# Forgetting attention moved into q's weight blocks, its query gate taken off TensorE, and two modulation chunks in other jobs

## The chip, the cores and the metric

The kernel is one program on one core of a Trainium2 chip. The metric is the device time of one execution in microseconds (us). A core has TensorE (PE; PEld is its weight load), VectorE (DVE), ScalarE (ACT), GpSimd (POOL) and SyncE (SP); each runs its own instruction stream in order, and the streams wait for one another by semaphores.

## The reference, cut to what matters

Batch 1, 256 tokens, width 2048, float32. A first block (an S5 state-space layer, then a forgetting-attention layer, "fox") is followed by a second block of two hybrid layers (retention beside latent attention), each modulated by a vector computed from `c`.

```python
# fox layer: 16 heads of 128; k, v, cum from shared_kv
s = einsum('bhqd,bhkd->bhqk', q_i, k) * dh ** -0.5
s = s + c_i[..., :, None] - cum[:, :, None, :]     # c_i: the queries' part of cum
s = where(kpos <= qpos, s, NEG_INF)
p = softmax(s, -1); o = p @ v
o = o * silu(z);  h = h + rmsnorm(o @ w_out, g_post)
# hybrid layer l
mod = silu(c) @ w_mod[l] + b_mod[l]                # 6144 values: shift, scale, gate
h = rms_norm(x, g) * (1 + scale) + shift
...
x = x + gate * out
```

`cum` is the running sum of the log forget gates, per head and token.

## The kernel before

**The weight stream.** Every big product is a job (`u`, `z`, `glu`, `s5out`, `k`, `v`, `f`, `q`, `foxz`, `foxout`, then per hybrid layer `rq`, `rk`, `rv`, `ga`, `rg`, `cq`, `ckv`, `kr`, `mg`, four groups of `uq`, `ukv`, `gb`, then `mlaproj`, `retproj`, `out`), and a job of width 2048 is 16 blocks of 128 output columns. SyncE loads each block's weights (1 MB) into one of four `raw` buffers. ScalarE rounds it to `whi` (L444), VectorE subtracts to get `wlo` (L903), two buffers each. TensorE multiplies, for each of the 16 k tiles, `whi` with `xs` hi and lo together (512 columns, L1562) and `wlo` with `xs` hi (256 columns, L1564) into `acc`. ScalarE copies the second half of `acc` out (`acctmp`, L468), VectorE adds the halves into the destination tile (L953). After block j both then split the weights of block j + 2.

**Side work.** `project(key, side=...)` calls `side(j)` on each engine after block j; this is how small work is laid between blocks. The order on each engine is the order written there.

**The modulation.** `MOD_JOBS` names twelve jobs. While such a job runs, VectorE adds one 128x1024 chunk of `w_mod`, scaled by `c`, per block to `modacc` (`mod_step`, L925; the first step after a `memset`, L940), GpSimd loads the chunks (L423), and at the job's end TensorE waits for the last step, sums `modacc` over partitions with 32 small matmuls into `bank[5]` (L1579), and VectorE adds the bias into `modv` (L962). `before_mod` is one more wait ahead of these matmuls where `bank[5]` is also used by attention. The chunks in order are shift, scale and gate of layer 0 (six), then of layer 1.

**Forgetting attention.** Sixteen heads go through `attend_slot(k)`, a software pipeline: slot k makes the scores of head k + 1 on TensorE (L1790 to L1792), the mask pass, maxima and negation of head k + 1 (L1052 to L1056) and the normalisation of head k (L1060 to L1062) on VectorE, the exponentials (L529) on ScalarE, the transposes of head k - 1 (L1619, L1622) and their copies (L537, L538), the product with v of head k - 2 (L1631, L1632), and its copy into `w3` on VectorE (L1356, which counts `att_stored`). Scores of one head are, for both query blocks of 128, three matmuls: q·k (L1790), the queries' part of `cum` spread over keys (L1791), and minus the keys' part spread over queries (L1792); each takes 128 columns for the first query block and 256 for the second.

All of `q` is projected first. Then ScalarE multiplies `w3` (q) by `FOX_SCALE` in four passes (L748), TensorE waits for these (`q_scaled`), slot -1 runs alone, and slots 0 to 15 follow the 16 blocks of `foxz` (the gate z, into `w1`). The gate is sigmoid (ScalarE, `zsig`, L756) and two multiplications (VectorE, L1035) for each group of four heads, three of them after blocks 7, 11 and 15. After `foxz` come slots 16 and 17, the last group's gate, and the four hi (L768) and four lo (L983) splits of the result into `xs`, which `foxout` reads.

**A pattern used elsewhere.** `glu` (and `mlaproj`, `retproj`) end otherwise: the first three groups of the next input are split during the job's last block (`before_last`), each as soon as TensorE has passed the k tiles that it overwrites (`x_released`, k = 3, 7, 11); the weight split of the last block is held back (`held`, `split_held`) behind the fourth group.

Of the kernel before, what the change touches and what calls it, by code (L numbers as in the profile page):

```python
# [69 lines left out]
MOD_JOBS = [(None, n) for n in ("glu", "s5out", "k", "v", "q", "foxz")] + \  # L70
           [(0, n) for n in ("rv", "ga", "rg", "mg", "mlaproj", "retproj")]
# [42 lines left out]
RELEASES = [(None, "glu"), (None, "f")] + [(l, n) for l in range(2) for n in ("mlaproj", "retproj")]  # L114
OVER = {n: f for n, _, f in NORMS}
SPLIT_GROUPS = dict(SPLITS)

# [3 lines left out]
def hybrid_program(nc, x_t, x_p, wstream, modstream, vecs, s5_adt, s5_b, s5_c, s5_cbd, s5_skip, fox_bf, positions,  # L121
# [3 lines left out]
    with ExitStack() as ctx:  # L125
# [70 lines left out]
        fcum = at("fcum", [P, 5, T], F32, o_cr)  # L196

# [239 lines left out]
        def _(act):  # L437
# [16 lines left out]
            def project(key, side=None, held=False):  # L454
                b0 = JOBS[key][0]

                def one(j, s):
                    piece, whole = pieces(key, j)
                    for t, par, _, q in tiles_of(key, j, s):
# [8 lines left out]
                        act.activation(acctmp[:, par % 2, :], acc[par % 2][:, T:2 * T], ACT.Copy).then_inc(acc_low_copied, 1)  # L468
# [267 lines left out]
            def forget(j):  # L736
# [5 lines left out]
                if j == 1:  # L742
                    act.wait_ge(sem("forget_1p"), 1)
                    act.activation(fcum[0:FOX_H, 1, :], fcum[0:FOX_H, 1, :], ACT.Ln).then_inc(sem("forget_ln"), 1)
            project((None, "q"), side=forget)
            act.wait_ge(acc_summed, JOBS[(None, "foxz")][1])
            for g in range(4):
                act.activation(group(w3)(g), group(w3)(g), ACT.Copy, scale=FOX_SCALE).then_inc(sem("q_scaled"), 1)  # L748
            attend_slot(0, -1, FOX_H)

            def z_gate(g):

                act.wait_ge(acc_summed, JOBS[(None, "foxz")][1] + 4 * g + 4)
                if g:
                    act.wait_ge(sem("silu_used"), g)
                act.activation(zsig[:, :, :], group(w1)(g), ACT.Sigmoid).then_inc(sem("silu_gate"), 1)  # L756

            def fox_side(j):
                attend_slot(0, j, FOX_H)
                if j in (7, 11, 15):  # L760
                    z_gate(j // 4 - 1)
            project((None, "foxz"), side=fox_side)
            attend_slot(0, FOX_H, FOX_H)
            z_gate(3)
            act.wait_ge(acc_done, JOBS[(None, "foxout")][1])
            for g in range(4):
                act.wait_ge(sem("silu_used"), g + 1)
                act.activation(xs[:, 4 * g:4 * g + 4, 0, :], group(w3)(g), ACT.Copy).then_inc(x_hi_done, 1)  # L768
# [3 lines left out]
            for l in range(2):  # L772
                silu0, gates0 = 4 + 8 * l, 8 * l
# [123 lines left out]
        def _(dve):  # L897
# [36 lines left out]
            def project(key, dest, rows=P, side=None, turn=lambda ap: ap, held=False):  # L934
# [7 lines left out]
                def one(j, s):  # L942
# [3 lines left out]
                    for t, par, jt, q in tiles_of(key, j, s):  # L946
                        if piece:
                            lo_piece(*piece, q)
                        if key == (None, "z"):
# [3 lines left out]
                        dve.tensor_tensor(out=dest(jt), in0=turn(acc[par % 2][0:rows, 0:T]), in1=turn(acctmp[0:rows, par % 2, :]),  # L953
                                          op=ALU.add).then_inc(acc_summed, 1)
# [90 lines left out]
            def attend_slot(a0, k, heads, scale, kind, finish):  # L1045

                if k + 1 < heads:
                    i, a = k + 1, a0 + k + 1
                    dve.wait_ge(sem("att_scores"), a + 1)
                    if a >= 2:  # L1050
                        dve.wait_ge(sem("att_turned"), a - 1)
                    link(dve.scalar_tensor_tensor(out=smx[:, i % 2, :], in0=bank[i % 2][:, 0:384], scalar=scale,  # L1052
                                                  in1=mask[:, kind, :], op0=ALU.mult, op1=ALU.add))
# [280 lines left out]
            def forget(j):  # L1334
# [4 lines left out]
                if j == 1:  # L1339
# [4 lines left out]
                    dve.tensor_scalar(F[4], F[2], -1.0, None, ALU.mult).then_inc(sem("cum_ready"), 1)  # L1344
            split_x("pre1", stg_half, xs, 3)
            split_held((None, "f"))
            project((None, "q"), lambda j: tile(w3, j), side=forget)
            dve.wait_ge(sem("masks_loaded"), 16)
# [6 lines left out]
            def fox_slot(k):  # L1355
                attend_slot(0, k, FOX_H, 1.0, 0, lambda i, o: dve.tensor_copy(w3[:, i, :], o))  # L1356

            def z_mul(g):
                dve.wait_ge(sem("att_stored"), 4 * g + 4)
                silu_mul(0, g, group(w1)(g), zsig[:, :, :], group(w3)(g))  # L1360

            def fox_side(j):
                fox_slot(j)
                if j in (7, 11, 15):
                    z_mul(j // 4 - 1)
# [693 lines left out]
```

## Time and profile before

| | us |
|---|---|
| median of three runs | 3378.76 (3378.43 to 3387.96) |
| the profiled execution, its own time | 3377.11 |
| its span, first to last instruction | 3375.4 |
| TensorE busy | 3165.9 (94%) |
| VectorE busy | 2237.6 (66%) |
| ScalarE busy | 1480.8 (44%) |
| the 16 DMA engines, mean rate | 193 GB/s |

Busy time is the union of an engine's instructions; mean granted TensorE clock was 0.976 of full speed (2.4 GHz). A timeline row gives start, duration and, in brackets, how long the engine sat idle before it and what released it. Matmuls overlap, so what one costs is the distance to the start of the next, not its duration.

### The profile page before, as it was taken

How to read it: one execution, taken by the hardware profiler on the slowest of the kernel's cores; microseconds unless marked ns; L12 is line 12 of the kernel's file. 1: busy time of each engine (PE TensorE's matmuls, PEld its weight loads, DVE VectorE, ACT ScalarE, POOL GpSimd, SP SyncE). 2: the span in 40 equal slices, each digit the busy share in tenths (PEclk: the TensorE clock that was granted, in tenths of full speed). 3: DMA queues.
4: the chain of work that ended last, by engine and by line, in shares of the span. 5: the costliest groups of instructions: out<-in, count | busy, mean ns of one | idle time of the engine just before them, and what ended most of it. 6: DMA issues, size and time to landing. Idle time of an engine off the chain costs nothing. (4 is left out here: it accounts for less than half of the span.)

```text
span 3375.4 us, 51760 instructions
## 1 busy us (share of the span) xinstructions
PE 3165.9 (94%) x20984; PEld 2734.9 (81%) x20984; DVE 2237.6 (66%) x2653; ACT 1480.8 (44%) x1843; POOL 108.0 (3%) x206
## 2 busy tenths in 40 slices
PE   6999997999989799999999999989999999999997
PEld 5898886878878688888877778868888887777886
DVE  7687877687674668677766667764555765565564
ACT  5454543344453333344444444433334544444443
POOL 0000000000000000000000000000000000000000
PEclk9999998999999899999999999989999999999999
DMA  5334764767544366656653467645544554344543
GB/s 209 127 112 147 260 245 167 280 249 264 187 160 153 145 219 256 235 213 242 244 187 134 149 250 288 217 181 176 179 157 162 188 199 173 127 150 176 212 175 112
DMA packets 102889, 650.13 MB, mean 193 GB/s; under 512 B 11552, under 2 KB 12704, under 8 KB 38688
## 3 DMA queue, kind: packets, MB, share of 16 engines
q1 hardware_dynamic: 71856, 512.44, 42.3%
q0 software_dynamic: 28528, 105.92, 8.7%
q10 hardware_dynamic: 2304, 28.84, 2.1%
q8 instruction: 157, 2.57, 0.3%
q14 instruction: 44, 0.36, 0.0%
HBM read 632.47 MB, written 14.68 MB: 192 GB/s over the span
## 5 line engine op out<-in xcount | busy, mean ns | idle before, releaser
L1562 PE MATMUL acc<-xs,whi 128*128 128x512 f32 x6960 | 2501.1, 403 | 76.3 <-DVE xs L983 60.2
L1564 PE MATMUL acc<-xs,wlo 128*128 128x256 f32 x6960 | 1957.1, 281 | 0.0
L1562 PEld LDWEIGHTS acc<-xs,whi 128*128 128x128 f32 x6960 | 1315.2, 189 | 407.5 <-issue 59.5
L903 DVE TENSOR_TENSOR wlo<-raw,whi 128x2048 fp32r<-128x2048 f32 x459 | 1051.8, 2292 | 502.0 <-ACT whi L444 501.4
L1564 PEld LDWEIGHTS acc<-xs,wlo 128*128 128x128 f32 x6960 | 1322.8, 190 | 6.2 <-issue 3.6
L444 ACT ACTIVATE whi<-raw 128x2048 fp32r<-128x2048 f32 x459 | 875.2, 1907 | 0.0
L468 ACT ACTIVATE acctmp<-acc 128x256 f32<-128x256 f32 x547 | 208.8, 383 | 1349.6 <-PE acc L1564 1331.4
L953 DVE TENSOR_TENSOR w<-acc,acctmp 128x256 f32<-128x256 f32 (+1 forms) x480 | 206.2, 430 | 462.9 <-ACT acctmp L468 462.3
L925 DVE SCALAR_TENSOR_TENSOR modacc<-modw,cact,modacc 128x1024 f32<-128x1024 f32 x192 | 245.6, 1279 | 16.0 <-DMA modw<-in_modstream 14.7
L423 POOL DMA_DIRECT2D modw<-in_modstream x192 | 101.5, 529 | 1709.7 <-DVE modacc L925 1037.4
L529 ACT ACTIVATE smx<-smx,stat 128x128 f32<-128x128 f32 x96 | 43.0, 448 | 175.6 <-DVE stat L1056 175.6
L1562 PE MATMUL acc<-cks,whi 128*128 128x512 f32 x256 | 92.5, 404 | 10.8 <-DVE wlo L916 10.8
L1557 PE MATMUL acc<-xs,whi 128*128 128x256 f32 x512 | 93.0, 284 | 2.2 <-DVE wlo L903 2.2
L1562 PE MATMUL acc<-cqs,whi 128*128 128x512 f32 x192 | 76.8, 436 | 19.1 <-DVE w L953 10.1
L1557 PEld LDWEIGHTS acc<-xs,whi 128*128 128x128 f32 x512 | 79.7, 192 | 2.5 <-DVE wlo L903 2.4
L1559 PE MATMUL acc<-xs,wlo 128*128 128x256 f32 x256 | 72.4, 283 | 0.0
L1564 PE MATMUL acc<-cks,wlo 128*128 128x256 f32 x256 | 71.7, 280 | 0.0
L1562 PEld LDWEIGHTS acc<-cks,whi 128*128 128x128 f32 x256 | 48.0, 188 | 26.7 <-DVE wlo L916 15.7
L916 DVE TENSOR_TENSOR wlo<-raw,whi 128x512 fp32r<-128x512 f32 (+1 forms) x80 | 63.7, 796 | 8.0 <-ACT whi L451 4.2
L1562 PEld LDWEIGHTS acc<-cqs,whi 128*128 128x128 f32 x192 | 39.7, 207 | 31.0 <-DVE w L953 11.4
L1564 PE MATMUL acc<-cqs,wlo 128*128 128x256 f32 x192 | 57.1, 297 | 0.0
L451 ACT ACTIVATE whi<-raw 128x512 fp32r<-128x512 f32 (+1 forms) x80 | 56.7, 709 | 0.0
(256 smaller groups left out, 2181.9 us busy)
## 6 DMA issues: line engine op xcount, KB each, us to landing
raw<-in_wstream SPq DMA_DIRECT2D x483, 1024.0 KB, 4.8
modw<-in_modstream POOLq DMA_DIRECT2D x192, 512.0 KB, 4.7
residual<-h ACTq DMA_DIRECT2D x2, 2048.0 KB, 6.3
ga_gate<-w ACTq DMA_DIRECT2D x2, 2048.0 KB, 10.9
gated_retention<-w ACTq DMA_DIRECT2D x2, 2048.0 KB, 8.5
w<-gated_retention ACTq DMA_DIRECT2D x2, 2048.0 KB, 8.2
h<-residual ACTq DMA_DIRECT2D x2, 2048.0 KB, 12.6
w<-ga_gate ACTq DMA_DIRECT2D x2, 2048.0 KB, 11.3
```

The source lines that it names most:

```text
L423: pool.dma_start(modw[s][:, :], src).then_inc(mod_loaded[s], 16)
L444: act.activation(whi[s % SPL][:, :], raw[slot][:, :], ACT.Copy).then_inc(w_hi_done, 1)
L451: ins = act.activation(whi[n % SPL][:, c], raw[n % RAW][:, c], ACT.Copy)
L468: act.activation(acctmp[:, par % 2, :], acc[par % 2][:, T:2 * T], ACT.Copy).then_inc(acc_low_copied, 1)
L903: dve.tensor_tensor(out=wlo[s % SPL][:, :], in0=raw[s % RAW][:, :], in1=whi[s % SPL][:, :].bitcast(F32), op=ALU.subtract).then_inc(w_lo_do ...
L916: ins = dve.tensor_tensor(out=wlo[n % SPL][:, c], in0=raw[n % RAW][:, c], in1=whi[n % SPL][:, c].bitcast(F32), op=ALU.subtract)
L925: dve.scalar_tensor_tensor(out=modacc[:, :], in0=modw[s % 2][:, :], scalar=cact[:, bass.ds(j, 1)] if not isinstance(j, int) else cact[:, j ...
L953: dve.tensor_tensor(out=dest(jt), in0=turn(acc[par % 2][0:rows, 0:T]), in1=turn(acctmp[0:rows, par % 2, :]), op=ALU.add).then_inc(acc_summ ...
L1557: pe.matmul(acc[par % 2][:, 0:T], whi[w][:, c:c + cols], x_split[:, k, a, :], start=(k == 0 and a == 0), stop=False, skip_group_check=True)
L1559: mm = pe.matmul(acc[par % 2][:, 0:T], wlo[w][:, c:c + cols], x_split[:, k, 0, :], start=False, stop=(k == kts - 1), skip_group_check=True)
L1562: pe.matmul(acc[par % 2][0:cols, :], whi[w][:, c:c + cols], x_split[:, k, :, :], start=(k == 0), stop=False, skip_group_check=True)
L1564: mm = pe.matmul(acc[par % 2][0:cols, 0:T], wlo[w][:, c:c + cols], x_split[:, k, 0, :], start=False, stop=(k == kts - 1), skip_group_check ...
```

## The change

1. Attention starts after block 3 of `q` (`FOX_FIRST`) with slot -1; slots 0 to 11 follow blocks 4 to 15 of `q`, slots 12 to 17 follow blocks 0 to 5 of `foxz`. TensorE's `q` job is now written out block by block.
2. The scale goes into q's sum (ScalarE's copy of the low half takes `scale`, VectorE's addition becomes a multiply-add), so the four passes L748 and `q_scaled` go.
3. The matmuls L1791 go. Instead TensorE transposes the queries' part of `cum` once (after block 2), VectorE copies 16 columns per query block into `cumcol`, and the mask pass adds its column as a per-partition scalar, in two passes (128 and 256 columns wide) for the former one of 384.
4. The gate of groups 0, 1 and 2 runs after blocks 4, 8 and 12 (ScalarE) and 5, 9 and 13 (VectorE) of `foxz`. In the last block's time the gate of three tiles of group 3 and the splits of groups 0 to 2 are made; the last tile's gate, the fourth group's split and the held weight split follow.
5. `foxz` and layer 0's `rg` no longer carry a modulation chunk; layer 1's `rv` and `mg` do. `before_mod` now stands at the end of `q`: it waits until head 9 is stored.

```diff
-MOD_JOBS = [(None, n) for n in ("glu", "s5out", "k", "v", "q", "foxz")] + \
-           [(0, n) for n in ("rv", "ga", "rg", "mg", "mlaproj", "retproj")]
+MOD_JOBS = [(None, n) for n in ("glu", "s5out", "k", "v", "q")] + \
+           [(0, n) for n in ("rv", "ga", "mg", "mlaproj", "retproj")] + [(1, "rv"), (1, "mg")]
...
+FOX_FIRST = 3
+FOX_SILU = 5
+def fox_slot_at(job, j):
+    return j - FOX_FIRST - 1 if job == "q" else KT - FOX_FIRST - 1 + j
...
# ScalarE
-                        act.activation(acctmp[:, par % 2, :], acc[par % 2][:, T:2 * T], ACT.Copy).then_inc(acc_low_copied, 1)
+                        act.activation(acctmp[:, par % 2, :], acc[par % 2][:, T:2 * T], ACT.Copy,
+                                       scale=FOX_SCALE if key == (None, "q") else 1.0).then_inc(acc_low_copied, 1)
...
-            for g in range(4):
-                act.activation(group(w3)(g), group(w3)(g), ACT.Copy, scale=FOX_SCALE).then_inc(sem("q_scaled"), 1)
...
+            def fox_hi(groups, key):
+                for g in groups:
+                    if key:
+                        act.wait_ge(sem("x_released"), released(key, g))
+                    act.wait_ge(sem("silu_used"), g + 1 if g < 3 else FOX_SILU)
+                    act.activation(xs[:, 4 * g:4 * g + 4, 0, :], group(w3)(g), ACT.Copy).then_inc(x_hi_done, 1)
+            def fox_early():
+                z_gate(3, range(3))
+                fox_hi(range(3), (None, "foxz"))
+            project((None, "foxz"), side=before_last(fox_side, fox_early), held=True)
+            z_gate(3, (3,), 1)
+            split_held((None, "foxz"))
             act.wait_ge(acc_done, JOBS[(None, "foxout")][1])
+            fox_hi((3,), None)
...
# VectorE
+                        if key == (None, "q"):
+                            dve.scalar_tensor_tensor(out=dest(jt), in0=acc[par % 2][:, 0:T], scalar=FOX_SCALE,
+                                                     in1=acctmp[:, par % 2, :], op0=ALU.mult, op1=ALU.add).then_inc(acc_summed, 1)
...
+                    if shift:
+                        for n, (lo, hi) in enumerate(((0, 128), (128, 384))):
+                            last = dve.scalar_tensor_tensor(out=smx[:, i % 2, lo:hi], in0=bank[i % 2][:, lo:hi], scalar=shift(n, i),
+                                                            in1=mask[:, kind, lo:hi], op0=ALU.add, op1=ALU.add)
+                        link(last)
...
+                if j == FOX_FIRST:
+                    dve.wait_ge(sem("masks_loaded"), 16)
+                    dve.wait_ge(sem("cum_turned"), 1)
+                    link(dve.tensor_copy(cumcol[:, :, :], bank[4][:, 0:T].rearrange("p (n q) -> p n q", n=2)[:, :, 0:FOX_H]))
+                if j >= FOX_FIRST:
+                    fox_slot(fox_slot_at("q", j))
...
+            def fox_early():
+                z_mul(3, range(3))
+                for g in range(3):
+                    fox_lo(g)
+            project((None, "foxz"), lambda j: tile(w1, j), side=before_last(fox_side, fox_early), held=True)
+            z_mul(3, (3,), 1)
+            fox_lo(3)
+            split_held((None, "foxz"))
...
# TensorE
+                pe.wait_ge(acc_summed, JOBS[(None, "q")][1] + i + 1)
                 for n, (lo, m) in enumerate(((0, P), (P, T))):
                     o = b[:, lo:lo + m]
                     pe.matmul(o, w3[:, i, n * P:(n + 1) * P], w1[:, i, 0:m], start=True, stop=False)
-                    pe.matmul(o, fcum[:, 2, n * P:(n + 1) * P], sel.to_broadcast([P, m]), start=False, stop=False)
                     mm = pe.matmul(o, sel.to_broadcast([P, P]), fcum[:, 4, 0:m], start=False, stop=True)
...
+            def q_side(j):
+                if j == 2:
+                    pe.wait_ge(sem("cum_ready"), 1)
+                    for n in range(2):
+                        mm = pe.transpose(bank[4][:, n * P:(n + 1) * P], fcum[:, 2, n * P:(n + 1) * P], ident[:, :])
+                    mm.then_inc(sem("cum_turned"), 1)
+                if j >= FOX_FIRST:
+                    fox_slot(fox_slot_at("q", j))
+            project((None, "q"), xs, fresh="pre1", side=q_side,
+                    before_mod=(sem("att_stored"), fox_slot_at("q", KT - 1) - 1))
```

## Rows read from the trace of the kernel before

**Rows 1.** The page's busy time of TensorE: us, share, instructions.

```profile
PE 3165.9 (94%) x20984; PEld 2734.9 (81%) x20984; DVE 2237.6 (66%) x2653; ACT 1480.8 (44%) x1843; POOL 108.0 (3%) x206
```

**Rows 2.** Busy windows, most of `foxz`: window, length, busy per engine, clock, DMA.

```profile
865.00:980.00 115.00, 115.00 (x697) 102.08 (x696) 82.17 (x146) 55.06 (x107) 6.96 (x14) 1.00 0.50 176
```

**Rows 3.** Timeline of TensorE, one slot and one block of `foxz`.

```profile
899.90 0.38 PE L1790 MATMUL bank<-w,w 128*128 128x128 f32 x2
900.12 0.39 PE L1791 MATMUL bank<-ident,fcum 128*128 128x128 f32 x2
900.35 0.39 PE L1792 MATMUL bank<-fcum,ident 128*128 128x128 f32 x2
...
901.00 0.60 PE L1791 MATMUL bank<-ident,fcum 128*128 128x256 f32 x2
901.44 0.59 PE L1792 MATMUL bank<-fcum,ident 128*128 128x256 f32 x2
901.87 0.38 PE L1619 MATMUL bank<-ident,w 128*128 128x128 f32 x2
...
902.99 0.48 PE L1562 MATMUL acc<-xs,whi 128*128 128x512 f32 x1
...
908.72 0.38 PE L1790 MATMUL bank<-w,w 128*128 128x128 f32 x2
```

**Rows 4.** Timeline of VectorE, the same slot and the block after it.

```profile
904.52 0.55 DVE L1052 SCALAR_TENSOR_TENSOR smx<-bank,mask 128x384 f32<-128x384 f32 x1
...
906.49 0.42 DVE L1356 COPY w<-bank 128x256 f32<-128x256 f32 x1
...
909.33 0.42 DVE L953 TENSOR_TENSOR w<-acc,acctmp 128x256 f32<-128x256 f32 x1 [1.24 <-ACT acctmp L468]
```

**Rows 5.** Timeline of TensorE, from `q`'s end to `foxz`'s first block.

```profile
851.62 0.71 PE L1579 MATMUL bank<-ones,modacc 128*32 128x1 f32 x64
857.53 0.79 PE L1790 MATMUL bank<-w,w 128*128 128x128 f32 x2 [5.20 <-ACT w L748]
...
860.94 0.58 PE L1562 MATMUL acc<-xs,whi 128*128 128x512 f32 x1
```

**Rows 6.** Timeline of TensorE, from `foxz`'s end to `foxout`'s second block.

```profile
996.42 0.38 PE L1619 MATMUL bank<-ident,w 128*128 128x128 f32 x2
...
1002.26 1.03 PE L1579 MATMUL bank<-ones,modacc 128*32 128x1 f32 x64 [4.48 <-DVE w L1356]
...
1018.36 0.39 PE L1562 MATMUL acc<-xs,whi 128*128 128x512 f32 x1
```

**Rows 7.** Timeline of TensorE and VectorE, `glu`'s end to `s5out`'s second block.

```profile
428.56 0.71 PE L1579 MATMUL bank<-ones,modacc 128*32 128x1 f32 x64 [0.26 <-DVE modacc L925]
...
428.42 3.49 DVE L983 TENSOR_TENSOR xs<-w,xs 128x1024 fp32r<-128x1024 f32 x3
...
439.21 0.71 PE L1562 MATMUL acc<-xs,whi 128*128 128x512 f32 x1
```

**Rows 8.** Timeline of TensorE, the end of layer 0's `ga`, then of `rg`.

```profile
1444.99 1.03 PE L1579 MATMUL bank<-ones,modacc 128*32 128x1 f32 x64 [3.98 <-DVE w L1415]
1445.96 0.79 PE L1562 MATMUL acc<-xs,whi 128*128 128x512 f32 x1
...
1454.05 1.89 PE L1876 MATMUL bank<-w,part 128*128 128x256 f32 x8
...
1558.24 1.03 PE L1579 MATMUL bank<-ones,modacc 128*32 128x1 f32 x64 [4.77 <-DVE modacc L925]
```

**Rows 9.** Busy windows: `rg` to `cq`, layers 0 and 1; `rv` to `ga`, likewise.

```profile
1454.30:1567.20 112.90, 107.86 (x641) 92.58 (x640) 85.09 (x64) 54.94 (x52) 7.40 (x14) 0.97 0.65 233
2573.60:2677.00 103.40, 103.35 (x576) 89.92 (x574) 67.10 (x48) 54.97 (x52) 0.00 (x0) 1.00 0.47 166
1240.80:1337.30 96.50, 96.50 (x593) 81.25 (x592) 78.37 (x74) 34.99 (x33) 8.46 (x16) 1.00 0.73 266
2367.80:2463.60 95.80, 95.71 (x528) 80.44 (x526) 59.24 (x56) 35.04 (x33) 0.00 (x0) 1.00 0.50 177
```

More of the change, by code:

```diff
@@ L113 @@
 NSQUARES = {n: k for n, k, _ in NORMS}
-RELEASES = [(None, "glu"), (None, "f")] + [(l, n) for l in range(2) for n in ("mlaproj", "retproj")]
+RELEASES = [(None, "glu"), (None, "f"), (None, "foxz")] + [(l, n) for l in range(2) for n in ("mlaproj", "retproj")]
 OVER = {n: f for n, _, f in NORMS}
 SPLIT_GROUPS = dict(SPLITS)
+FOX_FIRST = 3
+FOX_SILU = 5
+def fox_slot_at(job, j):
+    return j - FOX_FIRST - 1 if job == "q" else KT - FOX_FIRST - 1 + j
 ROPE_L = 8 + 1 + 2 * MLA_G
@@ L751, in z_gate @@
-            def z_gate(g):
-                act.wait_ge(acc_summed, JOBS[(None, "foxz")][1] + 4 * g + 4)
+            def z_gate(g, tiles=range(4), turn=0):
+                first = 4 * g + tiles[0]
+                act.wait_ge(acc_summed, JOBS[(None, "foxz")][1] + 4 * g + tiles[-1] + 1)
                 if g:
-                    act.wait_ge(sem("silu_used"), g)
-                act.activation(zsig[:, :, :], group(w1)(g), ACT.Sigmoid).then_inc(sem("silu_gate"), 1)
+                    act.wait_ge(sem("silu_used"), g + turn)
+                act.activation(zsig[:, tiles[0]:tiles[-1] + 1, :], w1[:, first:first + len(tiles), :], ACT.Sigmoid
+                               ).then_inc(sem("silu_gate"), 1)
@@ L1043, in rope, with attend_slot @@
                 tt(x, x, tmp, ALU.add).then_inc(rope_done, 1)
-            def attend_slot(a0, k, heads, scale, kind, finish):
+            def attend_slot(a0, k, heads, scale, kind, finish, shift=None):
                 if k + 1 < heads:
@@ L1354, in silu_mul, with z_mul, fox_lo @@
                 tt(x, x, gate, ALU.mult).then_inc(sem("silu_used"), 1)
-            def fox_slot(k):
-                attend_slot(0, k, FOX_H, 1.0, 0, lambda i, o: dve.tensor_copy(w3[:, i, :], o))
-            def z_mul(g):
+            def z_mul(g, tiles=range(4), turn=0):
                 dve.wait_ge(sem("att_stored"), 4 * g + 4)
-                silu_mul(0, g, group(w1)(g), zsig[:, :, :], group(w3)(g))
+                these = slice(4 * g + tiles[0], 4 * g + tiles[-1] + 1)
+                silu_mul(0, g + turn, w1[:, these, :], zsig[:, tiles[0]:tiles[-1] + 1, :], w3[:, these, :])
             def fox_side(j):
-                fox_slot(j)
-                if j in (7, 11, 15):
+                if fox_slot_at("foxz", j) <= FOX_H + 1:
+                    fox_slot(fox_slot_at("foxz", j))
+                if j in (5, 9, 13):
                     z_mul(j // 4 - 1)
-            fox_slot(-1)
-            project((None, "foxz"), lambda j: tile(w1, j), side=fox_side)
-            fox_slot(FOX_H)
-            fox_slot(FOX_H + 1)
-            z_mul(3)
-            for g in range(4):
-                dve.wait_ge(sem("silu_used"), g + 1)
-                split_x("foxgated", group(w3), xs, g)
+            def fox_lo(g):
+                dve.wait_ge(sem("silu_used"), g + 1 if g < 3 else FOX_SILU)
+                split_x("foxgated", group(w3), xs, g)
+            def fox_early():
[6 more added lines that the diff above has]
+            split_held((None, "foxz"))
             project((None, "foxout"), lambda j: tile(w1, j))
@@ L1378, in _ @@
             for l in range(2):
-                silu0 = 4 + 8 * l
+                silu0 = FOX_SILU + 8 * l
                 mv = modv[l]
```

51 lines of the change are left out of this document (24 added, 27 removed).

## The prediction

> **What bounds the kernel.** I read the page's busy times first. TensorE is busy 94% of the span [rows 1], so a gain must either take matmuls away or close one of its few gaps. Then the busy windows: through most of `foxz`, where attention runs now, TensorE is busy 115.00 of 115.00 us and VectorE 82.17 [rows 2]. So attention's matmuls are paid for in full there, and the VectorE and ScalarE work beside them is hidden. Then the timeline of TensorE around the stretch, to see what a slot and a block cost and where TensorE stands still: a slot lasts from 899.90 to 902.99, 3.09 us, and a block from there to 908.72, 5.73 us [rows 3]. The gaps are at `q`'s end, 5.20 us until ScalarE's scaling passes are done [rows 5], and at `foxz`'s end, where TensorE first waits 4.48 us for VectorE's copy of a head and then for the gate and the splits; `foxout`'s second block starts 21.94 us after the end of `foxz`'s last [rows 6]. Last I compared the same job with and without a modulation chunk by windows, for part 5 of the change [rows 9].
>
> **The change part by part.** The sum is made against the profiled execution's own time, 3377.1 us.
>
> *The query gate's matmuls.* L1791 costs TensorE 0.23 us (900.12 to 900.35) for 128 columns and 0.44 us (901.00 to 901.44) for 256, 0.67 us a head [rows 3]; 16 heads give 10.7 us. In their place come two transposes after block 2 and a 32-column copy on VectorE. The slot's five transposes and two products together take 1.12 us (901.87 to 902.99) [rows 3], so two transposes are bounded by 0 and 0.5 us; I take 0.3. Their wait for `cum_ready` lies a block after VectorE's scan; what is queued behind it is block 3, and a late scan would cost only its lateness.
>
> *Does TensorE stay the bound?* In `q` the slots meet a modulation step, as they do in `foxz` now, so the load per block on VectorE is the known one plus the second mask pass. VectorE now sits idle 1.24 us before it adds a block's halves [rows 4]. The block gets 0.67 us shorter, which leaves 0.57. The trace has no two-pass form. From below it costs 0 more, from above a whole pass of 0.55 us [rows 4]. A pass from PSUM takes 0.42 us for 256 columns and 0.55 for 384 [rows 4], which by a straight line is 0.29 for 128: 0.71 instead of 0.55, so I take 0.16 more and 0.4 us of spare. Even the upper end leaves 0.02 us. The Trainium skill, "VectorE: DVE Perf Modes", section on the TRN2 errata, gives an operation from PSUM a fixed term of 120 cycles at 0.96 GHz beside one cycle per element, an estimate of 0.13 us for the extra pass; the sum by it is the same. Adding the scale to VectorE's sum and ScalarE's copy adds no operand that is streamed, cost between 0 and the fixed part of a pass; I take 0. A head's scores now also wait for its q tile, which at slot k was added four blocks earlier: no cost. In `foxz` the chunk's steps go, so slots 12 to 17 have more room than they have today. The gate's passes there, two of about 1.16 us (3.49 for three, [rows 7]) after blocks 5, 9 and 13, lie beside a 5.7 us block whose weight work was made two blocks ahead: cost 0.
>
> *q's end.* Today `foxz`'s first block starts at 860.94; `q`'s last ended about 0.3 us before the sums of 851.62 [rows 5], as 0.26 us before them at `glu` [rows 7]. That is 9.6 us, of which slot -1's matmuls are worth 1.97 at full clock (899.90 to 901.87, [rows 3]): 7.7 us of pure loss. ScalarE's passes go, but `before_mod` moves the other wait here. After `q`'s last block TensorE runs slot 11 (3.09 - 0.67 = 2.4 us) and then waits for VectorE to copy head 9. In the row for this, that copy ends at 906.49 + 0.42, 7.0 us after the block's end at 899.90 [rows 3, 4]; with the second mask pass 7.2. So TensorE stands idle 4.7 us, as it does 4.48 at `foxz`'s end now [rows 6]. Behind the wait are the modulation sums and then `foxz`'s first block. Layer 0's `ga` ends just so: idle 3.98 us, sums 0.97, and a first block of 8.09 us (1445.96 to 1454.05) [rows 8] instead of 5.73, since it runs its first part at the lower clock level; 2.4 us. New loss 4.7 + 1.0 + 2.4 = 8.1 us, so this end **costs** 0.4 us. The stall is not removed, it changes its cause.
>
> *foxz's end.* Of today's 21.9 us [rows 6] slots 15, 16 and 17 are worth 1.12 + 1.12 + 0.6 = 2.8 at full clock and are still paid, after blocks 3 to 5. There remain 19.1. The new end is built like `glu`'s, where from the last block's end (428.56 - 0.26 = 428.3) to `s5out`'s second block at 439.21 it takes 10.9 us [rows 7], a block, the sums and the waits for the last group in it. The order differs in two places. Ahead of VectorE's three early splits stand two passes over three tiles (about 0.9 us each) in place of one modulation step (a pass over 1024 columns, about 1.2): 0.6 later. After the last tile two short passes (0.4 each) stand in place of one of 1.16: 0.3 earlier. I take 11.2 us. Behind ScalarE's three early hi splits is its copy of tile 15, behind VectorE's early work the sum of tile 15; both are in `glu`'s order as well, so in the 10.9. Gain 19.1 - 11.2 = 7.9 us.
>
> *The chunk out of layer 0's `rg`.* From `rg`'s first block to `cq`'s first it is 112.9 us in layer 0 with a chunk and 103.4 in layer 1 without [rows 9]. Of these 9.5 us I can name 4.77 idle before the sums [rows 8] (VectorE's step stands behind the group norm's reciprocal), 1.0 for the sums and up to 2.4 of lower clock after them, 8.1 in all. I take 8.8.
>
> *The chunks into layer 1's `rv` and `mg`.* `rv` takes 96.5 us with a chunk and 95.8 without [rows 9]: 0.7 us. From below 0, from above what `rg` showed, 9.5. In both jobs the long VectorE work of the last block stands after the last step, not before it as in `rg`, so I take 0.7 each, 1.4 us. Each step brings its load too, 16 a job on GpSimd's queue; with the chunk the DMA share in `rv` is 0.73 against 0.50 [rows 9], so SyncE's weights still have room.
>
> Sum: 10.7 - 0.3 - 0.4 + 7.9 + 8.8 - 1.4 = **25.3 us**, 3377.1 to 3351.8 us. The median of the runs lies 1.7 us above the profiled execution, so I forecast **3353.5 us**.
>
> **The rivals.**
>
> *The ends give nothing.* TensorE pays as much standing still at both ends as before, since VectorE's chain (gate of three tiles, three splits, sum, gate, split, weights) is longer than `glu`'s. For it: the wait at `q`'s end is already as long as the one removed. Against: `glu`'s row. Without the 7.5 us of both ends: 3361.
>
> *VectorE sets the pace in q.* If each slot's spare of 0.4 us is gone, TensorE waits and the 0.67 us come back in 15 of 16 slots, 10 us: 3363.5. For it: 0.02 us at the upper bound. Against: a late sum stops TensorE only two blocks on.
>
> *rg's wait stays.* TensorE then waits for VectorE's reciprocal anyway and only the sums' 1.0 us go: 3361. Against: in layer 1 without a chunk TensorE is busy 103.35 of 103.40 us [rows 9].
>
> *The clock falls twice at foxz's end.* TensorE has two waits there now; if it starts `foxout`'s first block at 1.2 GHz too, 2.4 us more as at `ga`'s end [rows 8]: 3356. The Trainium skill, "TensorE: Matmul & The Clock Gate", section on the HAM clock gate, holds that the slow level is the default and sustained activity lifts it, so that each long wait is paid again; by that rule this rival has its chance, and `ga`'s rows agree for a wait of 4 us.
>
> *Slower (the other side).* VectorE again, but for its whole slot: with the per-partition column each pass might cost far more than a pass with a constant. It decides from the 0.4 us of spare on; for 10 us over today it must lose 35 us in the 15 slots beside a block, 2.4 us each, so the pair of passes would have to take 3.5 us instead of 0.7: 3389. Nothing in the rows speaks for it.
>
> **How the numbers follow.** Forecast 0.67 (own range 3347 to 3359: the 8.1 to 9.5 of `rg`, 0 to 3 for the chunks, 2 either way for the ends); ends give nothing 0.10; VectorE sets the pace 0.08; `rg`'s wait stays 0.05; clock twice 0.05; slower 0.03; 0.02 for a larger gain. The range 3344 to 3364 takes in all but the last two and some spread of each. A measurement of this kernel tells about 0.3%, 10 us, from no change, so faster means under 3368.6: 0.93, within 0.04, slower 0.03.
>
> **What would show it.** In the profile after: slots of 2.4 us with no gap in `q` and busy TensorE to the last block; an idle of 4.7 us before L1579 at `q`'s end, released by the copy of a head, and a slow first block of `foxz`; `foxout`'s second block 11 us after `foxz`'s end; no gap before `cq` in layer 0; `rv` of layer 1 about 0.7 us longer. I am wrong if VectorE has no idle time left in `q`'s slots, or if TensorE idles inside blocks 4 to 15.

## The result, and the profile after

The changed kernel takes 3358.78 us (median of six runs, 3348.66 to 3360.59), the one before 3381.35 us in the six runs beside it (3375.82 to 3387.96). The ratio is 0.9927, with a 95% interval of 0.9909 to 0.9944: faster by 19 to 31 us, 22.6 by the medians, where 25.3 were forecast. The profiled execution took 3360.59 us. First the head of its page (busy us, share of the span, instructions):

```profile
span 3358.9 us, 51649 instructions
PE 3155.6 (94%) x20922; PEld 2726.3 (81%) x20922; DVE 2240.0 (67%) x2672; ACT 1472.7 (44%) x1836; POOL 108.1 (3%) x206
```

In these two profiles the span is 16.5 us shorter, less than the 22.6 between the medians. TensorE's busy time fell by 10.3 us, close to the 10.7 of the query gate's matmuls [rows 1]; the other 6.2 are idle time. To see where they lie, I cut every execution at the same marks, from ScalarE's first copy of a job's low half (L468 before, L478 after) to that of the next job:

```
us               before   after   forecast, from the sum
q and foxz       253.7    238.0   17.9 less (q 102.1 to 132.1, foxz 151.6 to 105.9)
rg, layer 0      112.9    103.0    8.8 less
rv, layer 1       95.7     98.2    0.7 more
mg, layer 1       91.1     91.6    0.7 more
```

That is 15.7 + 9.8 - 2.5 - 0.5 = 22.5 us in the jobs that the change touches. That it equals the difference of the medians is chance: the other jobs, which no edit touched, take 6.0 us more in this profile (`u`, the first job, 3.4 of them), so the spans differ by 16.5 only. Now the places one by one. Busy windows of the kernel after (start:end, length, then busy us and count of PE, PEld, DVE, ACT, POOL, granted clock, DMA share, GB/s): the slots in `q` and layer 0's `rg`:

```profile
800.00:878.00 78.00, 78.00 (x475) 69.28 (x474) 61.20 (x119) 37.28 (x78) 4.75 (x9) 1.00 0.55 196
1444.40:1547.40 103.00, 102.97 (x576) 89.79 (x574) 67.02 (x48) 54.94 (x51) 0.00 (x0) 1.00 0.46 158
```

TensorE is busy in all 78.00 us of the slots in `q`: VectorE has kept its room. `rg` runs without a gap, like layer 1's [rows 9]. The chain of TensorE's waits between 766 and 1005 us (which tile it waited for, who released it: us in total, times, the longest) names all that is left around attention:

```profile
PE acc L1608 <- DVE xs L1009: 4.7, 2, 2.6
PE bank L1625 <- DVE w L1385: 4.7, 1, 4.7
PE bank L1843 <- DVE fcum L1376: 1.9, 1, 1.9
PE acc L1608 <- DVE wlo L925: 1.0, 1, 1.0
```

The timeline of TensorE at the same places; the second to sixth rows are one slot, the seventh to ninth `q`'s end, and the last four `foxz`'s end:

```profile
781.26 0.44 PE L1843 MATMUL bank<-ident,fcum 128*128 128x128 f32 x2 [1.92 <-DVE fcum L1376]
...
842.27 0.38 PE L1834 MATMUL bank<-w,w 128*128 128x128 f32 x2
842.49 0.39 PE L1835 MATMUL bank<-fcum,ident 128*128 128x128 f32 x2
842.71 0.60 PE L1834 MATMUL bank<-w,w 128*128 128x256 f32 x2
843.14 0.59 PE L1835 MATMUL bank<-fcum,ident 128*128 128x256 f32 x2
843.58 0.38 PE L1665 MATMUL bank<-ident,w 128*128 128x128 f32 x2
...
885.06 0.38 PE L1678 MATMUL bank<-ptx,vtx 128*128 128x128 f32 x2
890.11 1.03 PE L1625 MATMUL bank<-ones,modacc 128*32 128x1 f32 x64 [4.67 <-DVE w L1385]
891.07 0.79 PE L1608 MATMUL acc<-xs,whi 128*128 128x512 f32 x1
...
993.65 0.28 PE L1610 MATMUL acc<-xs,wlo 128*128 128x256 f32 x1
995.97 0.47 PE L1608 MATMUL acc<-xs,whi 128*128 128x512 f32 x1 [2.03 <-DVE xs L1009]
...
1003.00 0.50 PE L1608 MATMUL acc<-xs,whi 128*128 128x512 f32 x1 [2.64 <-DVE xs L1009]
...
1005.21 0.80 PE L1608 MATMUL acc<-xs,whi 128*128 128x512 f32 x1 [0.48 <-DVE wlo L925]
```

- A head's four score matmuls now take 842.27 to 843.58, 1.31 us, against 899.90 to 901.87, 1.97 us, for six [rows 3]: 0.66 us less, 0.67 forecast.
- `q`'s end is as forecast: slot 11, then 4.67 us idle until VectorE has copied head 9, 0.96 us of sums, and a slow first block. That block lasts from 891.07 to 898.69, 7.6 us. The old end's 5.20 us [rows 5] are gone, and this wait stands in its place.
- `foxz`'s last block ends at 993.93; `foxout`'s second block starts at 1005.21, 11.3 us later (forecast 11.2; before 21.9 [rows 6]).
- New and not forecast: 1.92 us before the transposes of `cum`. In this profile the granted clock then falls to half inside the block behind them:

```profile
782.60:786.00 3.40, 3.40 (x13) 2.92 (x12) 3.40 (x3) 0.00 (x0) 0.53 (x1) 0.50 0.86 304
```

VectorE's rows in `q` for the mask pass (`x2`: both passes), for a head's copy and for a block's sum:

```profile
838.83 0.74 DVE L1080 SCALAR_TENSOR_TENSOR smx<-bank,cumcol,mask 128x128 f32<-128x128 f32 x2
...
840.98 0.42 DVE L1385 COPY w<-bank 128x256 f32<-128x256 f32 x1
...
842.88 0.42 DVE L976 SCALAR_TENSOR_TENSOR w<-acc,acctmp 128x256 f32<-128x256 f32 x1 [0.29 <-ACT acctmp L478]
```

The two passes take 0.74 us together, 0.19 more than the one [rows 4] (forecast 0.16), and the sum with the scale in it the same 0.42 us as a copy of that shape: nothing for the scale. VectorE still stands idle 0.28 to 0.39 us before it in the slots of `q`, near the 0.4 forecast and far from the 0.02 of the upper bound.

### The profile page after: what moved, and what is told of

Read it like the earlier page. It is cut to its first block and busy times, and to the rows that moved or that the text cites. A ratio compares the mean times of both kernels' runs of the same rounds, so it can differ in the third digit from the quotient of the medians.

```text
span 3358.9 us, 51649 instructions
## 1 busy us (share of the span) xinstructions
PE 3155.6 (94%) x20922; PEld 2726.3 (81%) x20922; DVE 2240.0 (67%) x2672; ACT 1472.7 (44%) x1836; POOL 108.1 (3%) x206
## 5 line engine op out<-in xcount | busy, mean ns | idle before, releaser
L478 ACT ACTIVATE acctmp<-acc 128x256 f32<-128x256 f32 x547 | 209.4, 384 | 1342.5 <-PE acc L1610 1324.1
L979 DVE TENSOR_TENSOR w<-acc,acctmp 128x256 f32<-128x256 f32 (+1 forms) x464 | 199.3, 430 | 459.2 <-ACT acctmp L478 458.8
L1608 PE MATMUL acc<-cks,whi 128*128 128x512 f32 x256 | 92.5, 404 | 10.7 <-DVE wlo L938 10.7
L1608 PEld LDWEIGHTS acc<-cks,whi 128*128 128x128 f32 x256 | 48.0, 188 | 26.6 <-DVE wlo L938 15.6
## 6 DMA issues: line engine op xcount, KB each, us to landing
ga_gate<-w ACTq DMA_DIRECT2D x2, 2048.0 KB, 11.3
w<-ga_gate ACTq DMA_DIRECT2D x2, 2048.0 KB, 10.4
```

Of the source, the lines that this page charges most:

```text
L1608: pe.matmul(acc[par % 2][0:cols, :], whi[w][:, c:c + cols], x_split[:, k, :, :], start=(k == 0), stop=False, skip_group_check=True)
```

## The experiments

Ten kernels, in three groups, each group on one chip together with the kernel before. "Before with ..." starts from the old kernel, "changed with ..." from the new one. The changed kernel itself ran twice more as a control: 3357.3 us (ratio 0.9940, 0.9925 to 0.9955) and 3355.02 us (0.9923, 0.9910 to 0.9938). They ran in the first group (part 3, part 2 and the chunk, each alone in the kernel before) and in the third (the gate behind the last block, `ga`'s sums, both banks). The second group had no run of the changed kernel on its chip, so its kernels are compared through the ratio to the kernel before, with both controls. Profiles are compared job by job.

### Control runs of the changed kernel

No edit.

> The changed kernel as it stands, as a control on the same chip. Ratio to before 0.9927 again, within its interval (0.991 to 0.994), 19 to 30 us faster. Both theories say the same; it is there so that the single parts and the whole are compared on one chip. If the parts add up, b_gate, b_scale and b_chunk give 9, 5 and 8 us, and what is left of the whole is the end of foxz (8 us) less the new wait at q's end.

> The changed kernel once more, as the control for the two versions of it beside it. 19 to 25 us faster than before, as twice seen.

Both agree with the result, 20 and 26 us faster than before by their ratios. Layer 1's `rv` takes 96.5 and 96.6 us in them (95.7 before, 98.2 in the first profile), the first job `u` 150.8 and 154.3 (151.1 before, 154.6 in the first profile). The difference of 1.6 us in `rv` is one of pace (last section): the starts of its pairs of matmuls lie 347 ns apart in the controls, as before, and 353 ns in the first profile. At the same pace the chunk there costs 0.8 to 1.0 us. In `u`, which no edit touched, the granted clock falls to half for some 3.4 us in the two longer profiles and stays at full speed in the two shorter ones, which is worth about half of the 3.5 us between them.

### Before with part 3 alone

```diff
+            def q_side(j):
+                if j == 2:
+                    pe.wait_ge(sem("cum_ready"), 1)
+                    ...two transposes of fcum into bank[4]
-                    pe.matmul(o, fcum[:, 2, n * P:(n + 1) * P], sel.to_broadcast([P, m]), start=False, stop=False)
...
+                        for n, (lo, hi) in enumerate(((0, 128), (128, 384))):
+                            last = dve.scalar_tensor_tensor(out=smx[:, i % 2, lo:hi], in0=bank[i % 2][:, lo:hi], scalar=shift(n, i), ...
```

> The kernel before with part 3 alone: no query-gate matmuls, cum turned once after q's block 2, the mask pass in two with the column added; attention stays beside foxz. Theory (TensorE is the bound in the slots): each slot is 0.67 us shorter, 10.7 less 0.3 for the transposes and up to 1.9 for their wait, so 8.5 to 10.4 us faster than before, VectorE idle before the addition of the halves down from 1.24 to about 0.4 us. Rival (VectorE paces the slots once TensorE is lighter, or the matmuls lay in time that TensorE had over): slots stay near 8.8 us with the block, no more than 3 us faster.

3378.96 us, ratio 1.0001 (0.9989 to 1.0012): within 4 us of nothing, where 8.5 to 10.4 us were expected. TensorE's waits from 760 to 1025 us in this kernel, and the rows around the second one on TensorE, ScalarE and VectorE:

```profile
PE bank L1807 <- ACT w L750: 5.2, 1, 5.2
PE bank L1631 <- ACT vtx L540: 4.2, 2, 2.1
PE bank L1797 <- DVE fcum L1352: 2.1, 1, 2.1
...
945.17 0.44 PE L1631 MATMUL bank<-ident,w 128*128 128x128 f32 x2 [2.09 <-ACT vtx L540]
...
933.28 1.28 ACT L758 ACT_TABLE_LOAD   x1
934.57 1.06 ACT L758 ACTIVATE zsig<-w 128x1024 f32<-128x1024 f32 x1
937.73 1.28 ACT L531 ACT_TABLE_LOAD   x1
...
944.75 0.37 ACT L540 ACTIVATE vtx<-bank 128x256 f32<-128x256 f32 x1
...
935.73 1.23 DVE L1037 TENSOR_TENSOR zsig<-zsig,w 128x1024 f32<-128x1024 f32 x1 [3.15 <-ACT zsig L758]
```

With the gate of a group between the slots, ScalarE loads a table for the sigmoid and one back for the exponential, VectorE waits 3.15 us for the sigmoid and then makes two passes, and the slot's transposes come late: TensorE waits 2.1 us after two of the three groups. In the kernel before TensorE had no gap there [rows 2]; its slots were longer and gave VectorE and ScalarE the time, by this reading, which the next kernel tests. Part 3 alone shortens a block only as long as nothing beside it is longer, and it adds 2.1 us for `cum`. By the marks `q` and `foxz` together are 2.5 us shorter, too little for the times to show.

### The same, with the gate of groups 0 to 2 behind the last block

```diff
-                if j in (7, 11, 15):
-                    z_gate(j // 4 - 1)
+                if j == 15:
+                    for g in range(3):
+                        z_gate(g)
```
and VectorE's two multiplications alike.

> The kernel before with part 3 alone, and the gate of z for groups 0 to 2 all after foxz's block 15 instead of after 7, 11 and 15. It tests why part 3 alone gave so little. Theory (the gate's ScalarE and VectorE passes in the slots made TensorE wait 2.1 us twice): no wait of TensorE inside blocks 7 to 12, from foxz's first block to its last about 4 us less than with the gate in the slots (15 blocks of 8.1 us); the end of foxz gets 5 us or more longer, so the whole is no faster. Rival (VectorE's second mask pass is what TensorE waits for): the two waits of 2 us stay somewhere in the slots.

One run, 3369.7 us (span 3368.0), which decides nothing by itself. Busy windows of the last blocks with slots, first for part 3 alone, then for this kernel:

```profile
871.00:995.00 124.00, 119.78 (x719) 105.42 (x718) 97.28 (x182) 62.72 (x124) 6.88 (x13) 1.00 0.53 183
```

```profile
865.00:984.00 119.00, 119.00 (x720) 105.65 (x719) 93.17 (x178) 56.23 (x118) 6.88 (x13) 1.00 0.55 191
```

The same TensorE work takes 119 us without a gap in place of 124: the gate among the slots was the cause. `foxz` from its first to its last block takes 129.6 us before, 124.3 with part 3 and 119.5 here; those are the 10 us. Most of it goes again at the end, where the three gates now stand bare (from the last block to `foxout`'s first 29.4 us, 23.4 with part 3, 21.9 before), and `q` and `foxz` together take 251.6 us, against 251.1 with part 3 alone and 253.7 before.

### Changed with part 3 undone

```diff
+                    pe.matmul(o, fcum[:, 2, n * P:(n + 1) * P], sel.to_broadcast([P, m]), start=False, stop=False)
...
-                attend_slot(0, k, FOX_H, 1.0, 0, lambda i, o: dve.tensor_copy(w3[:, i, :], o),
-                            shift=lambda n, i: cumcol[:, n, i:i + 1])
+                attend_slot(0, k, FOX_H, 1.0, 0, lambda i, o: dve.tensor_copy(w3[:, i, :], o))
```
The transposes stay, unused.

> The changed kernel with part 3 undone: the query-gate matmuls back in every slot and the mask pass in one; the transposes and the copy of cum stay, unused. In the kernel before, part 3 alone gave 0 to 3 us, since the gate of z in the slots after blocks 7 and 11 made TensorE wait 2.1 us each. Theory: in the changed kernel no gate of z falls among the slots, so the matmuls are worth their full 0.67 us each; 9 to 11 us slower than the changed kernel, ratio to before 0.9965 to 0.9975. Rival (the part never gave much): 0 to 4 us slower than the changed kernel.

3367.94 us, ratio 0.9957 (0.9940 to 0.9974), 6 to 11 us above the controls. By the marks, `q` takes 139.7 us against 130.4 and 130.2 in the controls and `foxz` 106.9 against 105.9 and 104.9: 10.2 and 11.5 us. VectorE here stands idle 1.23 us before a block's sum:

```profile
848.70 0.42 DVE L976 SCALAR_TENSOR_TENSOR w<-acc,acctmp 128x256 f32<-128x256 f32 x1 [1.23 <-ACT acctmp L478]
```

So in the changed kernel, where the gates run beside the last two slots or beside none, the matmuls are worth the full 10.7 us that were forecast, within what two controls tell, and the spare that they leave is the old 1.24 [rows 4].

### Before with part 2 alone

```diff
-            for g in range(4):
-                act.activation(group(w3)(g), group(w3)(g), ACT.Copy, scale=FOX_SCALE).then_inc(sem("q_scaled"), 1)
...
-            pe.wait_ge(sem("q_scaled"), 4)
+            pe.wait_ge(acc_summed, JOBS[(None, "foxz")][1])
```
with the scale in `q`'s sum as in the change.

> The kernel before with part 2 alone: the scale in q's sum, no scaling passes, TensorE waits for q's last tile only. Theory: the 5.2 us idle at q's end shrinks to the sum of the last tile (about 1 us) and the low clock after it is not met, 5 to 6.5 us faster. So moving attention into q is not what closes this gap; the changed kernel has another wait in its place (head 9's copy, 4.7 us idle). Rival (the gap is a wait for something else that is late too, such as the cum scan or the modulation sums): the idle stays above 3 us and the time within 2 us of before.

3376.39 us, ratio 0.9997 (0.9986 to 1.0008): nothing that the times show; the rival held. By the marks `q` is 1.3 us shorter (100.8 us). `q`'s end in this kernel, TensorE, then VectorE:

```profile
854.65 0.71 PE L1581 MATMUL bank<-ones,modacc 128*32 128x1 f32 x64 [0.15 <-DVE modacc L923]
859.26 0.53 PE L1792 MATMUL bank<-w,w 128*128 128x128 f32 x2 [3.90 <-DVE modv L964]
...
856.75 2.29 DVE L901 TENSOR_TENSOR wlo<-raw,whi 128x2048 fp32r<-128x2048 f32 x1 [1.37 <-ACT whi L444]
858.96 0.16 DVE L964 TENSOR_TENSOR modv<-bank,vec 128x8 f32<-128x8 f32 x1
```

Of the 5.20 us idle, 3.90 stay. The wait was covered twice: once ScalarE's passes are gone, TensorE waits for `bank[5]`, which VectorE frees only with its addition of `modv`, and that stands behind the weight split of 2.29 us.

### Before with the chunk taken out of layer 0's rg

```diff
-           [(0, n) for n in ("rv", "ga", "rg", "mg", "mlaproj", "retproj")]
+           [(0, n) for n in ("rv", "ga", "mg", "mlaproj", "retproj")] + [(1, "rv")]
```

> The kernel before with one chunk moved: from layer 0's rg to layer 1's rv. Theory: rg to cq takes 103 us instead of 113 and rv to ga 0.7 to 2 us more, in all 7 to 9 us faster. Rival (layer 0's rg is slow for a reason of its own, such as its place after ga's late end): rg keeps 110 us or more and the kernel is within 2 us of before.

3374.53 us, ratio 0.9982 (0.9970 to 0.9994): 2 to 10 us faster, 7 to 9 expected. `rg` takes 103.0 us in place of 112.9, as in the changed kernel, and layer 1's `rv` 96.4 in place of 95.7.

### Changed with the chunk back in layer 0's rg

```diff
-           [(0, n) for n in ("rv", "ga", "mg", "mlaproj", "retproj")] + [(1, "rv"), (1, "mg")]
+           [(0, n) for n in ("rv", "ga", "rg", "mg", "mlaproj", "retproj")] + [(1, "rv")]
```

> The changed kernel with one chunk back in layer 0's rg, and none in layer 1's mg. Theory: rg to cq 113 us again instead of 103, mg 0 to 1 us shorter; 8 to 10 us slower than the changed kernel, the same size as the one chunk gave in the kernel before (6 us by the runs). Rival (its worth hangs on the other parts): less than 4 us.

3366.95 us, ratio 0.9965 (0.9952 to 0.9978), 8 to 14 us above the controls. `rg` takes 113.1 us again, and TensorE's waits from 1400 to 1560 us show the two ends, `rg`'s and `ga`'s:

```profile
PE bank L1625 <- DVE modacc L947: 4.7, 1, 4.7
PE bank L1625 <- DVE w L1461: 4.0, 1, 4.0
```

Part 5's move is thus worth about 10 us in `rg` whichever kernel it is made in, less 0.5 to 1.0 for each job that takes a chunk. `mg` of layer 1 is 89.8 us here without it and 91.7 in the controls, but at two paces. At 353 ns a pair it takes 91.1 us without a chunk (before) and 91.6 to 91.7 with one, at 347 ns 89.8 to 89.9 without and 90.4 with one (in the kernels with part 3 undone and with `foxz`'s end as before).

### Changed with foxz's end as before

```diff
-            project((None, "foxz"), side=before_last(fox_side, fox_early), held=True)
-            z_gate(3, (3,), 1)
-            split_held((None, "foxz"))
+            project((None, "foxz"), side=fox_side)
+            z_gate(3)
...
-            fox_hi((3,), None)
+            fox_hi(range(4), None)
```
and VectorE's part alike.

> The changed kernel with the end of foxz as before: the whole fourth group's gate and all four hi and lo splits after the last block, the weight split not held. Attention still ends at block 5. Theory: from foxz's last block to foxout's second TensorE idles through the gate of group 3 and the splits, about 9 us against the 5.1 us it idles now; 3 to 5 us slower than the changed kernel. So of the 7.9 us I gave to this end about half is the slots that no longer stand there. Rival (grouping is the whole gain there): 8 us slower or more.

3361.47 us, ratio 0.9943 (0.9927 to 0.9959), 1 to 7 us above the controls: the times don't decide it. The trace does: from the end of `foxz`'s last block to `foxout`'s second it is 16.3 us in place of 11.3. By the marks `foxz` takes 111.5 us in place of 105.9 and 104.9, of which `foxout`'s second block gives back 1.9 and 0.8; in all 3.7 and 4.9 us against the controls, within the 3 to 5 expected. TensorE at the end, and two windows of `foxout`'s first block (the granted clock is the third number from the right):

```profile
991.63 0.28 PE L1602 MATMUL acc<-xs,wlo 128*128 128x256 f32 x1
1000.13 0.77 PE L1600 MATMUL acc<-xs,whi 128*128 128x512 f32 x1 [8.22 <-DVE xs L1005]
...
1000.10:1002.60 2.50, 2.47 (x7) 2.12 (x8) 2.50 (x3) 0.00 (x0) 0.00 (x0) 0.50 0.25 105
1002.60:1008.00 5.40, 5.40 (x25) 4.70 (x24) 0.78 (x1) 0.00 (x0) 0.00 (x0) 0.74 0.00 0
```

One wait of 8.22 us, then half clock (1.2 GHz). The changed kernel waits 2.03, 2.64 and 0.48 us. Its windows, one from `foxout`'s first block and one from the second, show that it isn't spared the low level either:

```profile
995.90:1000.40 4.50, 4.40 (x24) 3.63 (x24) 3.38 (x5) 1.94 (x2) 0.00 (x0) 1.00 0.26 111
1005.20:1007.60 2.40, 2.40 (x7) 2.11 (x8) 1.04 (x2) 2.05 (x2) 0.00 (x0) 0.50 0.48 116
```

The first block begins at full clock after 2.03 us of idle, the second begins at half clock, some 2.7 us of it. The clock falls once here, not twice. In the profiles of the other kernels with this end it falls once as well, in the first block or at the second's start, or not at all: in the second control and in the kernel of the next section it stays at full speed.

### Changed with q's modulation sums in another bank

```diff
+def sums_at(key):
+    return {(None, "q"): (1, 384)}.get(key, (5, 0))
...
-                            mm = pe.matmul(bank[5][rows, j:j + 1], ...
+                            mm = pe.matmul(bank[mb][rows, mc + j:mc + j + 1], ...
...
-            project((None, "q"), xs, fresh="pre1", side=q_side,
-                    before_mod=(sem("att_stored"), fox_slot_at("q", KT - 1) - 1))
+            project((None, "q"), xs, fresh="pre1", side=q_side)
```
`bank[1]` holds the scores of every other head in its first 384 columns; the sums go to columns 384 to 391, so nothing has to be copied out first.

> The changed kernel with q's modulation sums in another PSUM bank (bank 1, columns 384 to 391, free since the last score pass in it), so that they don't wait for head 9's copy; nothing else. Theory: the idle 4.7 us before the sums goes, and with it the low clock of foxz's first block (2 us): from q's last block to foxz's first 9 us instead of 16, 6.5 to 7.5 us faster than the changed kernel. Rival (as the kernel with the scale alone taught, the next wait stands right behind: VectorE's addition into modv, or the weights): TensorE idles 3 us or more after the sums or before slot 12, and the gain is under 3 us.

3348.03 us, ratio 0.9898 (0.9880 to 0.9917): 8 to 14 us faster than the controls, from four runs and with no control on this chip. From `q`'s last mark to `foxz`'s first it is 8.9 us against 15.8 and 15.5 in the controls, 6.6 to 6.9 less, within the 6.5 to 7.5 expected. `q` as a whole takes 125.1 us against 130.2 and 130.4, only 5.2 less, since in this profile the clock falls after the wait for `cum` and in the controls it doesn't (1.5 us). The times show more than this end; what the rest is, no trace says. TensorE at `q`'s end:

```profile
889.25 0.39 PE L1685 MATMUL bank<-ptx,vtx 128*128 128x128 f32 x2
889.57 0.71 PE L1632 MATMUL bank<-ones,modacc 128*32 128x1 f32 x64
890.21 0.50 PE L1614 MATMUL acc<-xs,whi 128*128 128x512 f32 x1
```

No idle time; the sums take 0.64 us in place of 0.96, and the block after them starts at once and at full clock. The wait that the change put at `q`'s end comes from the choice of bank alone.

### Changed with layer 0's ga sums in another bank

The same edit with `(0, "ga")` in place of `(None, "q")`.

> The changed kernel with layer 0's ga's sums alone in PSUM bank 1. Theory: from ga's last block to rg's first 8 us instead of 14.6, 6 to 7 us faster than the changed kernel. Rival: rg's first block or its first side work waits instead (the memset and VectorE's copy of the last head), 0 to 3 us.

3344.9 us, ratio 0.9895 (0.9880 to 0.9910), 9.5 us faster than the control on the same chip by the ratios, more than the 6 to 7 expected. `ga` takes 108.9 us against 115.8, 6.9 less; 5.5 of these lie at its end (7.8 us from its last mark to `rg`'s first, against 13.4), the other 1.4 are the faster pace of its blocks. Before, the end had 3.98 us of idle [rows 8], and 4.0 in the changed kernel; now:

```profile
1427.93 0.71 PE L1632 MATMUL bank<-ones,modacc 128*32 128x1 f32 x64
1428.57 0.50 PE L1614 MATMUL acc<-xs,whi 128*128 128x512 f32 x1
```

### Changed with both, and the transposes one block later

```diff
+    return {(None, "q"): (1, 384), (0, "ga"): (1, 384)}.get(key, (5, 0))
...
-                if j == 2:
+                if j == FOX_FIRST:
```

> The changed kernel with q's and layer 0's ga's modulation sums in PSUM bank 1 (each no longer waits for attention's or retention's last copy), and the transposes of cum after q's block 3 instead of 2. Theory: 9 us for q's end as measured, 4.0 idle and about 2.4 of low clock at ga's end, 1.9 of the wait for cum: 15 to 18 us faster than the changed kernel, 35 to 40 faster than the kernel before, ratio 0.988 to 0.9895. Rival (each wait taken away shows the next): no more than 10 us faster than the changed kernel.

3332.45 us, ratio 0.9857 (0.9842 to 0.9872): 49 us faster than before, and by the medians 22.6 faster than the control on the same chip. It beats both kernels. That is more than the 15 to 18 us expected, and the traces don't bear out the surplus. Its page's head, and the longest of TensorE's two groups of waits from 766 to 1020 us (the other is one wait of 0.3 us):

```profile
span 3335.7 us, 51647 instructions
...
PE acc L1614 <- DVE xs L1015: 4.7, 2, 2.6
```

The waits for `cum` and for head 9 are gone. Against that control's profile the three places give 1.8 us (up to `q`'s fourth mark, for `cum`), 6.5 (`q`'s end) and 5.5 (`ga`'s end), 13.8 in all, of 22.9 between the spans. `foxz` gives 2.2 back (slower pace, and the clock falls within `foxout`'s first block). The rest is the sum of jobs that no edit touched: `u` 4.4 us shorter, `z` 1.5, and parts of a microsecond in many. So 14 us are located, and the other 9 are not explained by these edits.

## Why the prediction was right, and where not

**The query gate's matmuls (10.7).** Right: 0.66 us a head; undoing it costs 10.2 to 11.5 in the traces. What the forecast didn't say is that it needs part 4, the gates moved: alone it gives nothing.

**Transposes (0.3) and their wait (nothing).** This is the step that failed: "a late scan would cost only its lateness", and then the lateness was priced at nothing, without asking the trace when `cum` is ready. VectorE ends the forget chain at 781.2, TensorE asks 1.92 us earlier. The scan does lie a block ahead in VectorE's order, but it starts late, and the trace of before would have told: there TensorE ends block 2 of `q` at 777.26, and the chain's last pass on VectorE ends 2.1 us later.

```profile
779.05 0.28 DVE L1344 TENSOR_SCALAR fcum<-fcum 16x256 f32<-16x256 f32 x1
```

Nor did the lateness cost only itself. From `q`'s first mark to its fourth it is 18.8 us before and in the last experiment, where the transposes come one block later. It is 20.5 to 20.6 us in five profiles of the changed kernel and its variants, but 22.1 in the other three, the first profile among them, because there the clock falls to half behind the wait. So transposes and wait cost 1.7 to 1.9 us in five and 3.3 in three, not 0.3.

**VectorE stays off the path.** Right, with 0.28 to 0.39 us to spare where 0.4 was forecast. The extra pass costs 0.19 us. The 0.13 us estimated from the Trainium skill, "VectorE: DVE Perf Modes", section on the TRN2 errata, was a little low; the straight line through the rows, 0.16, was nearer.

**q's end (costs 0.4).** Right in its mechanism and nearly in size: idle 4.67 (4.7), sums 0.96 (1.0), a first block of 7.6 us (8.1) that begins at 1.2 GHz. By the marks this end takes 15.9 us with 2.4 of slot work in it, before 15.5 with 2.0, so it cost nothing rather than 0.4. The window of the kernel after, in the block behind the sums:

```profile
890.90:893.40 2.50, 2.50 (x26) 2.20 (x20) 0.17 (x1) 0.00 (x0) 0.00 (x0) 0.50 0.33 138
```

The other bank takes wait and low clock away together, so both came from that wait.

**foxz's end (7.9).** Right: 11.3 us against 11.2. The early gate and splits are worth 5.0 us of it. The other 3 belong to slots 15 to 17 standing in `foxz` now, or to the modulation sums that no longer stand between them behind their wait of 4.48 us [rows 6]; the expectation put them down to the slots alone, and no run parts the two.

**rg (8.8).** A little too small: 9.8 in the first profile, 9.5 in the controls. What I could name was 8.1, and the whole difference of the layers 9.5; the upper one was right.

**The chunks in layer 1 (1.4).** Right at the same pace of TensorE: 0.8 to 1.0 for `rv`, 0.5 to 0.6 for `mg`. The 2.5 us of `rv` in the first profile are mostly the other pace.

The total: of the 25.3 forecast the jobs concerned show 22.5 in the first profile (3.0 less for `cum`, 1.0 more for `rg`, 1.8 less for `rv`, and 0.2 to 0.5 more for each of `q`'s end, `foxz`'s end and `mg`) and 25.4 and 26.6 in the controls. The medians differ by 22.6, with an interval of 19 to 31. So the terms are borne out job by job; that the total came within 3 us is in part luck, since jobs that no edit touched move a single profile by 4 to 10 us. Of the rivals, none took place: `q`'s end stayed as long, as forecast, but `foxz`'s did not, VectorE didn't set the pace, `rg`'s wait went, the clock fell once at most at `foxz`'s end.

## What to carry to other kernels

When one resource is freed among others of nearly the same length, measure the parts in both directions: part 3 alone gave nothing, since the gate among the slots took over, yet undoing it in the full change cost 10 us; and part 2 alone gave nothing, since the wait was covered twice. For each wait that a moved step brings, look up in the old trace when its producer ends, and don't stop at the order of the instructions. And before a wait in front of a tiny product is accepted, ask whether it only guards a buffer: eight free columns elsewhere gave 5.5 to 6.9 us an end.

## What the runs showed of the hardware

Not expected: at full granted clock TensorE runs most blocks of the same work at one of two paces. Layer 0's and layer 1's `rq` and `rk` in one execution of the kernel before, identical work:

```profile
1152.00:1235.00 83.00, 83.00 (x481) 73.20 (x480) 40.76 (x30) 32.83 (x30) 0.00 (x0) 1.00 0.50 177
2277.00:2362.00 85.00, 85.00 (x483) 73.70 (x482) 40.77 (x30) 32.81 (x30) 0.00 (x0) 1.00 0.51 181
```

A pair of matmuls (512 and 256 columns) starts every 353 ns in some stretches and every 347 ns in others, 5.65 or 5.55 us a block. Which one a job gets changes between executions: `rq` of layer 0 takes 44.4 us before and 45.2 in the first profile after, `rv` with a chunk 96.5 or 98.1. What sets the pace wasn't found. It bounds what a single profile says of a job of 16 blocks: 1.6 us are within it, unless the pace is read beside the time. It does not make the spread between executions: the first control has 62 blocks at 347 ns and 180 at 353, the first profile after 87 and 158, and yet the control's span is 5.1 us the shorter.

Not expected either: a wait of 1.9 to 2.1 us, after more than 10 us of matmuls without a gap, was followed by half clock in some executions and not in others. That is the wait for `cum`: in three of the ten profiles that have it the granted clock falls to 0.50 behind it (the row at 782.60), and in the other seven it stays at 1.00. Where it falls, the wait costs 1.5 us more than it lasts.
